# Expert weights rounded and corrected in two halves each, with a wait for each half

## What is computed

```
def run_block(args):
    xblk, e = args
    return (jax.nn.silu(xblk @ w1[e]) * (xblk @ w3[e])) @ w2[e]
...
out = jnp.zeros((N + 1, D), yb.dtype).at[slot_tok].add(yb * slot_gate[:, None].astype(yb.dtype))
```

## Time and profile before

| | |
|---|---|
| median of three runs | 2383.85 us (2382.08 to 2384.18) |
| the profiled execution | 2383.99 us |
| its span in the trace | 2382.2 us |
| TensorE busy in the span | 2169.3 us, 91% |
| VectorE | 1640.2 us, 69% |
| ScalarE | 1231.9 us, 52% |
| GpSimd | 456.9 us, 19% |
| expert stage in the trace | from 1526 to 2321 us |

### The profile page before, as it was taken

One profiled execution on the slowest core, in us unless ns is written; L12 is line 12 of the kernel. 1 busy time (PEld: TensorE's weight loads), 2 busy tenths in 40 slices (PEclk: granted clock), 3 DMA queues, 4 the chain that ended last, 5 costly groups with the idle time before them and its releaser, 6 DMA issues. The chain is left out here.

```text
span 2382.2 us, 40662 instructions
## 1 busy us (share of the span) xinstructions
PE 2169.3 (91%) x13164; PEld 1826.7 (77%) x13165; DVE 1640.2 (69%) x2984; ACT 1231.9 (52%) x2031; POOL 456.9 (19%) x257
## 2 busy tenths in 40 slices
PE   7999999998898999999989998599999999999970
PEld 6899999897677777777878886477777878777850
DVE  5444444466777878777775886678788866767746
ACT  5333333323666766676662221266676655655536
POOL 0000000000100001001001111125454533334426
PEclk9999999999999999999999998699999999999985
DMA  4111222242000000000044333579999988888837
GB/s 183 63 62 62 77 78 73 103 150 85 6 6 7 18 6 17 7 7 10 6 152 147 141 141 132 202 304 366 331 380 340 371 278 274 299 275 281 288 73 280
DMA packets 83214, 361.85 MB, mean 152 GB/s; under 512 B 25808, under 2 KB 37840, under 8 KB 68112
## 3 DMA queue, kind: packets, MB, share of 16 engines
q1 hardware_dynamic: 70144, 318.88, 35.3%
q0 software_dynamic: 11520, 41.16, 7.5%
q10 hardware_dynamic: 1440, 0.37, 0.1%
HBM read 291.97 MB, written 68.94 MB: 152 GB/s over the span
## 5 line engine op out<-in xcount | busy, mean ns | idle before, releaser
L2327 DVE TENSOR_TENSOR w_raw<-w_raw,w_hi 128x4096 fp32r<-128x4096 f32 x64 | 282.3, 4413 | 0.0
L2238 ACT CAST w_hi<-w_raw 128x4096 fp32r<-128x4096 f32 x64 | 232.8, 3638 | 84.5 <-issue 42.9
L1172 POOL TENSOR_TENSOR qT_lo<-q_raw,qT_hi 128x512 fp32r<-128x512 f32 x32 | 40.9, 1278 | 1140.8 <-ACT qT_hi L1116 1140.8
L1134 ACT CAST prT_hi<-pT 128x512 fp32r<-128x512 f32 (+1 forms) x288 | 162.3, 564 | 147.0 <-PE pT L1038 145.8
L1254 DVE TENSOR_TENSOR prT_lo<-pT,prT_hi 128x512 fp32r<-128x512 f32 (+1 forms) x288 | 188.1, 656 | 56.6 <-ACT prT_hi L1134 54.6
L2139 PE MATMUL eH<-w_hi,at_tok 128*128 128x512 f32 x512 | 208.1, 406 | 7.0 <-DVE at_tok L2322 7.0
L2140 PE MATMUL eH<-w_hi,at_tok 128*128 128x512 f32 x512 | 205.3, 401 | 0.0
L1245 DVE TENSOR_REDUCE mx<-pS 128x1 f32<-128x512 f32 (+2 forms) x320 | 191.0, 608 | 13.6 <-PE pS L1028 7.0
L98 POOL TENSOR_TENSOR cell<-cell 128x1 f32<-128x1 f32 x66 | 95.0, 1439 | 450.8 <-DVE y L2340 376.2
L2327 DVE TENSOR_TENSOR w_raw<-w_raw,at_row 128x4096 fp32r<-128x4096 f32 x31 | 137.2, 4426 | 55.1 <-ACT at_row L2238 55.1
L1126 ACT ACTIVATE pr<-pS,nmx 128x512 f32<-128x512 f32 (+1 forms) x240 | 151.0, 639 | 36.6 <-DVE nmx L1249 36.3
(11 more groups left out here) (433 smaller groups left out, 5979.8 us busy)
## 6 DMA issues: line engine op xcount, KB each, us to landing
w_raw<-in_w SPq DMA_DIRECT2D x96, 2048.0 KB, 11.9
xt<-in_x SPq DMA_DIRECT2D x9, 1024.0 KB, 8.2
xs<-in_x SPq DMA_DIRECT2D x8, 1024.0 KB, 4.8
scratch_h<-hp SPq DMA_DIRECT2D x16, 512.0 KB, 2.7
scratch_z<-hp SPq DMA_DIRECT2D x16, 512.0 KB, 3.6
fz<-scratch_z SPq DMA_DIRECT2D x16, 512.0 KB, 7.4
out<-fz SPq DMA_DIRECT2D x16, 512.0 KB, 2.6
scratch_xT<-xT_hi SPq DMA_DIRECT2D x7, 1024.0 KB, 4.0
```

Source lines behind the costliest of these rows:

```text
L1134: nc.scalar.copy(ph[:, u % RING, 0:w], T[u % NTB][:, 0:w]).then_inc(t_hi, 1)
L2238: nc.scalar.copy(w.hi[:], w.words(side).bitcast(F32)).then_inc(w.hi_ready, 1)
L2327: v.tensor_tensor(w.words(side), w.words(side).bitcast(F32), w.hi[:].bitcast(F32), ALU.subtract).then_inc(w.lo_ready, 1)
```

## The change

All three weights of a round are cast and corrected in two halves of 128 x 2048. Each weight has two more semaphores, `hi_half` and `lo_half`, raised by the first half; `hi_ready` and `lo_ready` are now raised by the second. On ScalarE, w1's second half moves behind the casts of x (`split_first`), so x's casts stand between the halves; the halves of w3 and w2 follow each other. On VectorE the halves follow each other in each remainder's place, each after a wait for its own half of hi. On TensorE the products start after the first half, and the wait for the whole stands in the middle, before the first product that reads the second half. For w2, whose products run through two halves of the columns, the inner waits stand in the first run alone. `rest` is called ahead of the wait for the remainder and no longer behind it. The last w2 (`close`) is treated in the same way.

```
@@ first, on TensorE
-                        pe.wait_ge(w.hi_ready, r + 1)
+                        pe.wait_ge(w.hi_half, r + 1)
...
                         for k in range(KT):
+                            if k == KT // 2:
+                                pe.wait_ge(w.hi_ready, r + 1)
                             pe.matmul(H[:], xh[:, k, :], w.hi[:, k, :], start=(k == 0), stop=False)
                             pe.matmul(H[:], xl[:, k, :], w.hi[:, k, :], start=False, stop=False)
-                        pe.wait_ge(w.lo_ready, r + 1)
                         lo = rest(w, r)
+                        pe.wait_ge(w.lo_half, r + 1)
                         for k in range(KT):
+                            if k == KT // 2:
+                                pe.wait_ge(w.lo_ready, r + 1)
                             ins = pe.matmul(H[:], xh[:, k, :], lo[:, k, :], start=False, stop=(k == KT - 1))
...
@@ second, on TensorE
-                    pe.wait_ge(w2.hi_ready, r + 1)
+                    pe.wait_ge(w2.hi_half, r + 1)
                     for half in range(2):
                         at = slice(half * 512, (half + 1) * 512)
                         for k in range(K2):
+                            if half == 0 and k == K2 // 2:
+                                pe.wait_ge(w2.hi_ready, r + 1)
...
@@ ScalarE
-                    nc.scalar.copy(w.hi[:], w.words(side).bitcast(F32)).then_inc(w.hi_ready, 1)
+                    for half in range(2):
+                        at = slice(half * (w.k // 2), (half + 1) * (w.k // 2))
+                        nc.scalar.copy(w.hi[:, at], w.words(side)[:, at].bitcast(F32)).then_inc(w.hi_ready if half else w.hi_half, 1)
+
+                def split_first(r, side, half):
+
+                    at = slice(half * (KT // 2), (half + 1) * (KT // 2))
+                    if half == 0:
+                        act.wait_ge(w1.loaded[side], r * 8 - side * 8 + 16)
+                        if ever(r, 1):
+                            act.wait_ge(w13_free, r)
+                    nc.scalar.copy(w1.hi[:, at], w1.words(side)[:, at].bitcast(F32)).then_inc(w1.hi_ready if half else w1.hi_half, 1)
...
                     tails = Tails(act, r)
-                    split_hi(w1, r, side, w13_free, r)
+                    split_first(r, side, 0)
                     x_part(r)
+                    split_first(r, side, 1)
                     tails.of(tails.here, tails.after, x_tail)
@@ VectorE
-                    v.wait_ge(w.hi_ready, r + 1)
-                    v.tensor_tensor(w.words(side), w.words(side).bitcast(F32), w.hi[:].bitcast(F32), ALU.subtract).then_inc(w.lo_ready, 1)
+                    for half in range(2):
+                        at = slice(half * (w.k // 2), (half + 1) * (w.k // 2))
+                        v.wait_ge(w.hi_ready if half else w.hi_half, r + 1)
+                        v.tensor_tensor(w.words(side)[:, at], w.words(side)[:, at].bitcast(F32), w.hi[:, at].bitcast(F32),
+                                        ALU.subtract).then_inc(w.lo_ready if half else w.lo_half, 1)
```

More of the change, by code:

```diff
@@ L1905, in phase_e @@
         psum = lambda name, n=512: ctx.enter_context(nc.psum_tensor(name, [P, n], F32))
+        hi_half, lo_half = {}, {}
+        for name in ("w1", "w3", "w2"):
+            hi_half[name], lo_half[name] = sem(name + "_hi_half"), sem(name + "_lo_half")
         class Weights:
             def __init__(self, name, k, n):
+                self.hi_half, self.lo_half = hi_half[name], lo_half[name]
                 self.src = d[name]
@@ L2166, in second @@
                         for k in range(K2):
+                            if half == 0 and k == K2 // 2:
+                                pe.wait_ge(w2.hi_ready, r + 1)
                             pe.matmul(Y[half][:], uh[:, k, :], hi[:, k, at], start=(k == 0), stop=False)
                             pe.matmul(Y[half][:], ul[:, k, :], hi[:, k, at], start=False, stop=False)
-                    pe.wait_ge(w2.lo_ready, r + 1)
                     lo = rest(w2, r)
+                    pe.wait_ge(w2.lo_half, r + 1)
                     for half in range(2):
@@ L2173, in second @@
                         for k in range(K2):
+                            if half == 0 and k == K2 // 2:
+                                pe.wait_ge(w2.lo_ready, r + 1)
                             ins = pe.matmul(Y[half][:], uh[:, k, :], lo[:, k, at], start=False, stop=(k == K2 - 1))
@@ L2303, in close @@
                     act.wait_ge(t_h, end.here * len(H_DONE) + 1)
-                    nc.scalar.copy(last_hi, w2.words(side).bitcast(F32)).then_inc(w2.hi_ready, 1)
+                    for half in range(2):
+                        at = slice(half * (K2 // 2), (half + 1) * (K2 // 2))
+                        nc.scalar.copy(last_hi[:, at], w2.words(side)[:, at].bitcast(F32)).then_inc(w2.hi_ready if half else w2.hi_half, 1)
                 by_side(act, last, close)
@@ L2403, in close @@
                 def close(side):
-                    v.wait_ge(w2.hi_ready, last + 1)
-                    v.tensor_tensor(w2.words(side), w2.words(side).bitcast(F32), last_hi.bitcast(F32), ALU.subtract).then_inc(w2.lo_ready, 1)
+                    for half in range(2):
+                        at = slice(half * (K2 // 2), (half + 1) * (K2 // 2))
+                        v.wait_ge(w2.hi_ready if half else w2.hi_half, last + 1)
+                        v.tensor_tensor(w2.words(side)[:, at], w2.words(side)[:, at].bitcast(F32), last_hi[:, at].bitcast(F32),
+                                        ALU.subtract).then_inc(w2.lo_ready if half else w2.lo_half, 1)
                 by_side(v, last, close)
```

## The result

The changed kernel took 2363.76 us in the median (2358.34 to 2365.39, four runs) against 2384.01 us before; the ratio is 0.9909, with a 95% interval from 0.9896 to 0.9921. So the change saves about 21 us, 0.9%, where 16 were forecast. The median stands 1 us inside the forecast range. The direction was right and so were the places that the forecast named, but one place was missing, and the size was short by a quarter. The profiled execution took 2364.19 us (span 2362.4).

The account below looks back on a forecast made before the run. TensorE was taken as the bound, its idle or slow time the only gain. Opening 4.0, turns 10.0, second tails 2.3 and end 0.5 made 16.8, less 0.8: 16 off 2383.99 gives 2368.0 us, range 2362.8 (all upper ends) to 2377.5.

Parts of the forecast that it names:

- the turns of the rounds: TensorE's way from w3's remainder to the next x transposes; ten rounds lose 11.6 us, gain 10.0 (8 to 11.6).
- x's lead: x's casts 1.70 us earlier, so w3's remainder ends 0.9 earlier; 3.6 of the 11.6 us lost remain.
- The opening: Rounds 0 and 1, where TensorE waits for xl behind w1's cast: gain 4.0 us (2 to 6.3).
- The x chain's 1.70 us: On ScalarE, only half of w1's cast ahead of x starts each x chain 1.70 us earlier.
- the wait in mid-group: TensorE's last wait has four products behind it, not eight; 0.5 us for each of four rounds.
- The second tails: In four rounds the tail's second products wait for xl; x 1.7 us earlier gains all 2.3.
- The end: TensorE's 4.0 us wait at L2167, its sequencer running out of the loop; 0.5 us gained.
- The deduction of 0.8: Small stalls from fixed parts and fuller DMA in the nine rounds with least slack: 0.8 us (0 to 2).
- A: Rival: the rounds give nothing, while the other three places and 1.4 us of mid-round waits stay; 2375.8 us, chance 0.14.
- B: Rival: the opening alone gains, VectorE gives back the rest; 4 us or less, 2380 to 2384, chance 0.08.
- C: Rival: slower, a wait inside a group breaks TensorE's flow even when met; 2404 us at one exposed load each, chance 0.08.
- D: Rival: the halves come when both are wanted anyway; within 0.2%, 2384 us, chance 0.04.

Follow-up runs that it names:

- the kernel with u first: Changed kernel with the loop ended at the last round and, behind it, u taken before the older tail of y on ScalarE and VectorE: 2353.01 us.
- the later load: Changed kernel, but round 1's load of w3 waits until the gather for round 1 has landed: 2361.84 us, measured once.

## Why the prediction was short, and what of it was right

By the ratio the change saved 21.7 us, more than the 21.2 that all upper ends of the forecast add up to. Two steps of the sum failed. The first is a term put at nothing: w2's halves, of which the sum has only the cost, gave 2.3 us. The second is a size in the turns of the rounds: x's lead was said to leave 3.6 us of stalls standing there, and it left 2.0. The mechanism of the four places that were named is borne out. Place by place:

**1. The opening** (4.0 forecast, 4.65 measured). The x chain's 1.70 us came as worked out: 1.70 in each of the two rounds, and with the order undone the stretch went back to 46.54 us. The clock in round 1 did not come back as forecast. I wrote that under 1 us of idling is left there; it was 1.9, and the products ran slow once more. My own rows gave that figure: a wait of 3.56 us that gets 1.7 shorter is 1.86. It cost nothing, because the step behind it was right: VectorE's remainder of w1 held the round in either case. With the remainder 0.9 us earlier round 1 is 0.8 us shorter; with the gather's wait gone it is no shorter. A gather that is later still does cost, 1.7 us in the execution that waited 3.14 us for it. The rest of the 0.65 is round 0's: it took 16.40 us instead of 18.87, 2.47 less, of which x's chain is 1.70; the clock stood at 1.2 GHz over fewer of its products.

**2. The turns** (10.0 forecast). Rounds 2 to 17 gave 11.42. Counted from one L2178 to the next, as the prediction did, 0.6 of that lies in rounds 6, 13 and 17, which have tails, and belongs to w2's halves (with w2 whole the three are 0.20, 0.21 and 0.19 longer). The other 10.8 are the ten rounds that it named; without round 6's late gather, in the changed kernel's second trace, they gave 11.2. The cause was the right one: w3's remainder was forecast to end 14.9 us into a round without a tail and ends at 14.86, the cast of u holds it as was said, and the rounds take 18.04 us. The mis-sized term is what x's lead leaves standing. I had 1.2, 0.5, 0.8 and 1.1 us left in rounds 2, 7, 10 and 14, so 8.0 us gained by the lead, and 2.0 more from the wait in mid-group. The run that waits for the whole remainder has the lead and not that wait. Its ten rounds gave 9.6, and the wait in mid-group gives the 1.7 that are missing there: 0.3 to 0.5 in each of the four rounds, near the 0.5 that I took. So the lead was too small by 1.6 and the wait too large by 0.3. What is left is 0.2 (round 14 alone, by 0.16 in the next L2178).

**3. The second tails** (2.3). 0.74, 0.34, 0.77 and 0.73 in rounds 19, 22, 27 and 31: 2.6. The excess of start over start that I took from the rows (0.69, 0.28, 0.67, 0.66) was a little low in each.

**4. The end** (0.5). 118.79 us from round 31 against 119.82, 1.03, of which 0.73 is its second tail: 0.3. The reading of the 4.0 us as a sequencer that runs out of the loop is shown by the kernel that ends the loop.

**The term that was missing** is w2's halves. My sum has only the cost of its two more instructions. The prediction did name the chain in round 1, the tail's products of w3 behind VectorE's product behind w2's remainder, but did not follow it into the later rounds, where it stood about 0.2 us in the way in 12 rounds: 1.7 us in rounds 18 to 30 and 0.6 before, shown by the run with w2 whole. The trace of before had it: round 18 took 27.37 us there and takes 27.14 now, and the first tail product of w3 started 0.33 us after the one ahead of it, where it now starts 0.23 after it.

**The deduction of 0.8** for small new stalls had no row behind it. The new stall there is, the tail gather (0.4 us in round 6), is a matter of one execution or another. Summed: 0.65 for the opening, 1.4 for rounds 2 to 17 (0.6 of it w2's halves, and the late gather taken off), 0.3 for the second tails, 1.7 for w2's halves in rounds 18 to 30 and 0.8 for the deduction, less 0.2 for the end, make up the 4.6 between 16 and 20.64. The range's low end was built from the largest sizes of the places that I had, 21.2, and so had no room for a place I had not.

**Rivals.** A fell twice: the DMA share stayed at 1.01 while the rounds shortened, and x's place carried the turns. B fell with rounds 2 to 30 giving 15 us, and D with them. C fell with 1536 met waits at no cost. The Trainium skill (TensorE: Matmul & The Clock Gate, specification table) says that the queue pulls weight loads ahead of running matmuls. Met waits on the weight loads did not hinder that, as far as the 18.03 us of the round show. The fixed part of a ScalarE instruction: of the changed kernel, a half of 2048 elements is followed after 1733.51 - 1731.70 = 1.81 us on ScalarE's timeline in round 10,

```profile
1731.70 1.91 ACT L2262 CAST w_hi<-w_raw 128x2048 fp32r<-128x2048 f32 x1 [1.56 <-PE eX L2119]
1733.51 1.06 ACT L2245 CAST at_tok<-eX 128x512 fp32r<-128x512 f32 x2
```

With 2048 / 1.2 = 1.71 for the elements 0.10 is left, as taken from the earlier trace rows, where 4096 elements were followed after 3.51. The Trainium skill (VectorE: DVE Perf Modes, the section on the fixed latency of SBUF sources) would make it 0.19, an estimate from its 224 cycles; the measurement decides for 0.10 between the starts of instructions, though the 1.91 that one lasts has 0.20 in it, near the page's figure.

**What stays open.** Why TensorE's way from the last wait to the next round is half a microsecond shorter when the whole remainder comes earlier, and longer in rounds 2, 7 and 14 of the run with both halves ahead of x; what `rest` ahead of the wait has to do with it was not tried apart. It was not tried with the loop written out, which would take the turn of the loop away. Nor was the order alone tried: x's casts ahead of a whole cast of w1, with no weight in halves.

## What to carry to other kernels

Where an engine prepares a large operand and a small one that the bound engine wants first, the order in its queue was worth more here than the halving in the old order (three quarters of the gain went with it): halve the large one so that the small one can go between. A wait that only becomes true late costs twice, by the data and by the instructions that the sequencer still has behind it, so put the last true wait as deep into a group as the data allows; met waits cost nothing that could be seen here. When a chain is found in one round, look for it in every round of the same form before its term is left out of the sum.

## What the runs showed of the hardware

- A wait on a semaphore that is already met, ahead of each of the 48 products of x with w1 and w3, left a round at 18.03 us: under 1 ns each over 48, as far as the trace resolves.
- The turn of a long loop costs TensorE's sequencer time: in the kernel before it took 3.73 and 3.45 us from the end of w3's remainder to the next round where the loop turns (rounds 10 and 14), against 2.59 to 2.66 in seven rounds where it does not. Seven empty turns of the changed kernel's loop kept TensorE from its next product for 3.7 us, and ScalarE idled 2.7 us and VectorE 5.8 us at the same place.
- The DMA engines at a share of 1.01 still gave 378 instead of 372 GB/s when asked for more, and 441 in a stretch of 4 us at 1.04. A share of 1 did not mean that they were at their limit.
- TensorE idled 1.57 us before round 3 of the kernel before, and 1.60 us at the end of the kernel with u first, and stayed at 2.4 GHz; after 1.88 us in round 1 of the changed kernel, and 1.85 with the later load, products came 0.43 us apart, at 1.2 GHz. The length of the idle alone does not decide it: behind the last wait, of 2.91 to 2.96 us, the changed kernel had slow products from the first on in one execution and from about the third on in the other, and the kernel that waits for the whole remainder had none.
- One and the same gather of a tail's 64 rows, in round 1, was waited for 1.9 and 2.3 us in two executions of the changed kernel, and 2.3, 2.4 and 2.8 us in three of kernels that differ from it only elsewhere or by met waits.
